# A PEER layer on one core: 64 of 320 tokens leave TensorE's down stage, their rows of v are gathered by GpSimd's indirect DMAs and summed by VectorE

## The reference

```python
q = (xt @ peer_w_q).reshape(PEER_BLOCK, PEER_HEADS, 2, D_KEY_HALF)
v1, i1 = lax.top_k(einsum('thd,nd->thn', q[:, :, 0], keys1), 16)
v2, i2 = lax.top_k(einsum('thd,nd->thn', q[:, :, 1], keys2), 16)
cand_s = v1[..., :, None] + v2[..., None, :]          # 16 x 16 candidates
best_s, pos = lax.top_k(cand_s, 16)                   # 16 experts, 8 heads
gate = jax.nn.softmax(best_s, axis=-1)
act = jax.nn.gelu(einsum('thkd,td->thk', peer_u[idx], xt))
return einsum('thk,thkd->td', gate * act, peer_v[idx])
```

## Time and profile before

| | |
|---|---|
| time before | 1413.51 us, median of 3 runs (1412.66 to 1414.91) |
| the profiled execution | 1415.16 us, its span 1413.4 us |
| busy, TensorE matmul | 1376.3 us, 97% of the span, 11325 instructions |
| busy, VectorE | 991.8 us, 70% |
| busy, ScalarE | 684.1 us, 48% |
| busy, GpSimd | 506.5 us, 36% |
| DMA | 168.69 MB, mean 119 GB/s |
| granted TensorE clock, mean | 0.997 |

### The profile page before, as it was taken

How to read it: one execution, slowest core, us unless ns; L and a number is a source line. 1 busy time by engine, 2 the same in 40 slices (tenths; PEclk the granted TensorE clock), 3 DMA queues, 4 the chain that set the end, 5 groups by cost and what they waited for, 6 DMA issues and landing times.

```text
span 1413.4 us, 34628 instructions
## 1 busy us (share of the span) xinstructions
PE 1376.3 (97%) x11325; PEld 1313.6 (93%) x11325; DVE 991.8 (70%) x2303; ACT 684.1 (48%) x1454; POOL 506.5 (36%) x672
## 2 busy tenths in 40 slices
PE   8999999989999999999999999999999999999996
PEld 6977787788999999999999999999999999999995
DVE  5348777767699995888888888856555555555556
ACT  4665544324445666444444444444444444444444
POOL 5000022302649998766666666652000000000000
PEclk9999999999999999999999999999999999999998
DMA  4343110013414545544444444445555555554553
GB/s 139 120 141 93 50 57 3 3 39 135 135 62 141 141 140 142 134 120 119 119 119 121 122 120 119 119 135 150 149 150 149 150 148 149 148 148 148 148 149 96
DMA packets 85288, 168.69 MB, mean 119 GB/s; under 512 B 9914, under 2 KB 11466, under 8 KB 85034
## 3 DMA queue, kind: packets, MB, share of 16 engines
q1 hardware_dynamic: 85226, 167.84, 40.8%
HBM read 164.80 MB, written 2.97 MB: 119 GB/s over the span
## 4 chain that ended last, share of the span: by engine, by line
PE 84%; POOL 5%; DVE 4%; issue 4%; ACT 2%; DMA 1%; SPq 0%; POOLq 0%; DVEq 0%; ACTq 0%
PE PS L1055 23%; PE PS L1057 22%; PE PS L1056 22%; POOL hlo L642 5%; PE PS L1488 5%; PE PS L1151 1%; PE PS L1335 1%; PE PS L1337 1%; PE PS L1320 1%; PE PS L1443 1%; PE PS L1050 1%; PE PS L1062 1%; DVE wlo L1570 1%; DVE XF L1570 0%; DVE states L1570 0%
## 5 line engine op out<-in xcount | busy, mean ns | idle before, releaser
L642 POOL TENSOR_TENSOR hlo<-hraw,hhiq 128x256 fp32r<-128x256 f32 x512 | 397.8, 787 | 144.8 <-ACT hhiq L690 142.6
L1055 PE MATMUL PS<-H1h,hhiq 128*128 128x320 f32 x1024 | 343.8, 336 | 3.4 <-POOL hlo L642 3.1
L690 ACT ACTIVATE hhiq<-hraw 128x256 fp32r<-128x256 f32 x508 | 210.9, 417 | 258.1 <-PE PS L1057 230.8
L1057 PE MATMUL PS<-H1h,hlo 128*128 128x320 f32 x1024 | 315.4, 308 | 0.0
L1056 PE MATMUL PS<-H1l,hhiq 128*128 128x320 f32 x1024 | 315.1, 308 | 0.0
L1057 PE MATMUL PS<-Wh,hlo 128*128 128x320 f32 x1016 | 314.0, 309 | 0.0
L1055 PEld LDWEIGHTS PS<-H1h,hhiq 128*128 128x128 f32 x1024 | 193.6, 189 | 9.3 <-POOL hlo L642 6.8
L1056 PEld LDWEIGHTS PS<-H1l,hhiq 128*128 128x128 f32 x1024 | 193.4, 189 | 0.0
L1057 PEld LDWEIGHTS PS<-H1h,hlo 128*128 128x128 f32 x1024 | 192.2, 188 | 0.0
L1057 PEld LDWEIGHTS PS<-Wh,hlo 128*128 128x128 f32 x1016 | 190.7, 188 | 0.0
L2011 DVE TENSOR_SCALAR oh<-iotak,pair 128x128 f32<-128x128 f32 x320 | 128.2, 401 | 48.4 <-PE PS L1488 43.8
(11 more groups left out here) (342 smaller groups left out, 2644.8 us busy)
## 6 DMA issues: line engine op xcount, KB each, us to landing
hraw<-in_uT SPq DMA_DIRECT2D x256, 256.0 KB, 2.6
hraw<-in_vE SPq DMA_DIRECT2D x254, 256.0 KB, 2.6
wraw<-in_wbig SPq DMA_DIRECT2D x50, 512.0 KB, 3.9
xin<-in_xT SPq DMA_DIRECT2D x4, 336.0 KB, 4.2
out_yT<-XF SPq DMA_DIRECT2D x8, 160.0 KB
ckx<-in_ckT SPq DMA_DIRECT2D x2, 512.0 KB, 6.9
vs<-in_cv SPq DMA_DIRECT2D x1, 768.0 KB, 8.2
out_ko<-kx SPq DMA_DIRECT2D x1, 672.0 KB
```

The costliest lines, as they stand in the source:

```text
L642: nc.gpsimd.tensor_tensor(hlo[q // 2 % 4][:, cols_], hraw[q // 2 % 4][:, cols_], hhiq[q % 4][:].bitcast(F32), ALU.subtract).then_inc(s_hlo ...
L690: return nc.scalar.activation(out, in_, f, **kw)
L1055: mm(out, whi_, xhi, start=start, stop=False)
L1057: return mm(out, wlo_, xhi, start=False, stop=stop)
```

## The change

The 64 decoding tokens (TM = 256 is where they begin) leave W, the grid and the down matmuls. The 128 experts that each of them picked are taken one by one instead.

- **Scores and routing**: the third set of 128 tokens held the last 128 before. Now both halves of the partitions hold the same 64 decoding tokens (two 64-partition matmuls for one), and later heads 0 to 3 are taken from the lower half, heads 4 to 7 from the upper. So 64 columns (HD = 64) of indices cover 64 tokens x 128 experts.
- **Up**: TensorE still computes all 320 columns. ScalarE takes the gelu of 256 columns as before, and that of the other 64 into a buffer `gd`, which its own DMA queue writes to a scratch tensor `gsc` in memory (one DMA of 32 KB for each e, issued one e later). There are 64 grid groups, not 80.
- **Down**: the matmuls have 256 columns. GpSimd gathers the activations with 64 indirect DMAs (one number for each of 128 partitions), and rows of v with 128 more (512 numbers for each partition, two for one index column). VectorE multiplies activation and gate, and from e = 48 on adds a row after four of five expert rows: 64 `scalar_tensor_tensor` of 1024 columns into `Ys`.
- **End**: eight float32 matmuls with a matrix `fold` add the two halves of the partitions of `Ys` into columns 256 to 320 of the PSUM banks.

```diff
+            def rows_of(n):
+                for x in range(2):
+                    nc.gpsimd.indirect_dma_start(vr[n % 4][:, 512 * x:512 * x + 512], None, vE.rearrange("a p c -> (a p) c"),
+                                                 bass.IndirectOffsetOnAxis(vix[x][:, n:n + 1], 0)).then_inc(s_vr[n % 4], 16)
+            pool.wait_ge(s_ys, 1)
...
+            for x in range(4):
+                pool.wait_ge(s_row[x], GELUS_OUT)
+            for n in range(HD):
+                nc.gpsimd.indirect_dma_start(acts[:, n:n + 1], None, gsc.rearrange("e i (t o) -> (e i t) o", o=1),
+                                             bass.IndirectOffsetOnAxis(aix[:, n:n + 1], 0)).then_inc(s_vr[0], 16)
+            for n in range(4):
+                rows_of(n)
             pool.wait_ge(s_down, 2)
...
+            for n in range(4, HD):
+                pool.wait_ge(s_ys, n - 1)
+                rows_of(n)
```

```diff
-                up_ = PS[:, slot % 4, 0:TQ]
-                A(W[:, bass.ds(e, 1), :].rearrange("p a t -> p (a t)") if direct else up_, up_, ACT.Gelu).then_inc(s_gelu, 1)
+                up_ = PS[:, slot % 4, 0:TM]
+                A(W[:, bass.ds(e, 1), :].rearrange("p a t -> p (a t)") if direct else up_, up_, ACT.Gelu)
...
+                A(gd[:, slot % 4, :], PS[:, slot % 4, TM:TQ], ACT.Gelu).then_inc(s_gelu, 1)
+                if not isinstance(e, int) or e > 0:
+                    keep_gelu(e - 1, slot - 1)
+            def keep_gelu(e, slot):
+                act.wait_ge(s_gelu, e + 1)
+                nc.scalar.dma_start(gsc[bass.ds(e, 1)].rearrange("a p t -> (a p) t"), gd[:, slot % 4, :]).then_inc(s_row[slot % 4], 16)
```

```diff
+                            for c in CHUNKS:
+                                ins = mm(out[c, :], QT[:, 2 * h + x, TM:TQ], kst[:, x, :], start=True, stop=True)
...
-                        ins = three(PS[:, 4 * b + kk, 0:TQ], hhv[2 * s + b][:, P * kk:P * kk + P], lo_[:, P * kk:P * kk + P],
+                        ins = three(PS[:, 4 * b + kk, 0:TM], hhv[2 * s + b][:, P * kk:P * kk + P], lo_[:, P * kk:P * kk + P],
                                     Wh[s][:], Wl[s][:], start, stop)
                         if stop:
-                            ins.then_inc(s_fin, 1)
+                            j = 4 * b + kk
+                            mm(PS[:, j, TM:TQ], Ys[:, P * j:P * j + P], fold[:], start=True, stop=True).then_inc(s_fin, 1)
...
+            pe.wait_ge(s_rconst, 2)
+            pe.wait_ge(s_ys, HD + 2)
```

```diff
+            v.memset(Ys[:], 0.0).then_inc(s_ys, 1)
+            with dve.Fori(1, VFROM // 2) as k:
                 for e in range(2):
                     down(k * 2 + e, e)
+            dve.wait_ge(s_vr[0], ACTS_IN[0] + 32)
+            own(tt(coef[:], acts[:], gat[:], ALU.mult))
+            with dve.Fori(1, (NI - VFROM) // VPER + 1) as k:
+                y = 0
+                for x in range(VPER):
+                    down(k * VPER + (VFROM - VPER + x), x % 2)
+                    if x % 5 < 4:
+                        dve.wait_ge(s_vr[y % 4], k * 64 + (ACTS_IN[y % 4] + 32 * (y // 4) - 32))
+                        dve.wait_ge(s_ys, k * 8 + (y - 6))
+                        v.scalar_tensor_tensor(Ys[:], vr[y % 4][:], coef[:, bass.ds(k * 8 + (y - 8), 1)], Ys[:], ALU.mult,
+                                               ALU.add).then_inc(s_ys, 1)
+                        y += 1
```

More of the change, by code:

```diff
@@ L57 @@
 RIT = 4
-NGR = TQ // 4
+TM = TQ - DEC
+NGR = TM // 4
+VFROM, VPER = 48, 10
 GATED, PAIRED, GRID0 = 9, 10, 11
@@ L250, in build @@
         cand = ranked.put("cand", [P, 3, 16, 16])
+        few = Region(BASE + NK * TM * 4, BASE + 134464)
+        rank = few.put("rank", [P, HD])
+        aix = few.put("aix", [P, HD], U32)
+        vix = [few.put(f"vix{i}", [P, HD], U32) for i in range(2)]
+        gat = few.put("gat", [P, HD])
+        acts = few.put("acts", [P, HD])
+        coef = few.put("coef", [P, HD])
+        fold = few.put("fold", [P, HD])
+        mid = Region(BASE + 134464, BASE + 154944)
+        gd = mid.put("gd", [P, 4, DEC])
+        Ys = mid.put("Ys", [P, D])
+        vr = [mid.put(f"vr{i}", [P, D]) for i in range(3)]
+        vr.append(at("vr3", [P, D], BASE + 154944))
+        gsc = nc.dram_tensor("gsc", (NI, P, DEC), F32, kind="Internal").ap()
         routing = Region(hole_at, TAIL)
@@ L423, in build @@
         s_vhi, s_vlo, s_wh, s_wl, s_down = (sem(x) for x in ("s_vhi", "s_vlo", "s_wh", "s_wl", "s_down"))
+        s_row = s_x
+        X_DONE, GELUS_OUT = 16, 16 + 16 * NI // 4
+        s_vr, ACTS_IN = [sem(f"s_vr{i}") for i in range(4)], (16 * HD, 0, 0, 0)
+        s_ys = sem("s_ys")
         s_sum, s_yf = sem("s_sum"), sem("s_yf")
@@ L664, in _ @@
                     lo(k * (4 * RIT) + q, q)
+            def rows_of(n):
[3 more added lines that the diff above has]
+            pool.wait_ge(s_ys, 1)
+            own(nc.gpsimd.memset(fold[:], 0.0))
+            for c in (0, HD):
+                select(fold[:], [[-1, HD]], ALU.not_equal, -c, 1, 1.0)
+            nc.gpsimd.sem_inc(s_rconst, 1)
+            for x in range(4):
[5 more added lines that the diff above has]
+                rows_of(n)
             pool.wait_ge(s_down, 2)
@@ L975, in _ @@
             up_rest(0)
-            with act.Fori(1, GATED) as k:
+            up_rest(1, blank=True)
+            with act.Fori(2, GATED) as k:
                 up_rest(k, blank=True)
@@ L1439, in scores_of_head @@
                     pe.wait_ge(s_scev, h - 2)
-                for u, t0 in enumerate((0, P, TQ - P)):
+                for u in range(3):
                     for x in range(2):
                         out = flat(PS, 512 * (2 + 2 * (h % 3)) + (2 * u + x) * NK, NK)
-                        ins = mm(out, QT[:, 2 * h + x, t0:t0 + P], kst[:, x, :], start=True, stop=True)
+                        if u < 2:
+                            mm(out, QT[:, 2 * h + x, P * u:P * u + P], kst[:, x, :], start=True, stop=True)
+                        else:
+                            for c in CHUNKS:
+                                ins = mm(out[c, :], QT[:, 2 * h + x, TM:TQ], kst[:, x, :], start=True, stop=True)
                 ins.then_inc(s_scp, 1)
@@ L1505, in _ @@
                     pe.wait_ge(s_routed, 2)
-                for tt in range(3):
+                for tt in range(2):
                     ins = nc.tensor.transpose(PS[:, 4 + x, P * tt:P * tt + P],
@@ L1544, in _ @@
                     down(k * 2 + e, e, False, False)
-            for e in range(NI - 2, NI):
-                down(e, e % 2, False, e == NI - 1)
+            down(NI - 2, 0, False, False)
+            pe.wait_ge(s_rconst, 2)
+            pe.wait_ge(s_ys, HD + 2)
+            down(NI - 1, 1, False, True)
             pe.wait_ge(s_onesg, 2)
@@ L1993, in _, with ranks @@
             v.tensor_copy(gsum[:], b3[:, :, 0]).then_inc(s_routed, 1)
+            sides = [(c, slice(4 * i, 4 * i + 4)) for i, c in enumerate(CHUNKS)]
+            def ranks(by):
+                for c, hs in sides:
+                    ins = v.scalar_tensor_tensor(rank[c, :], sel[c, 5, hs, :].rearrange("p h k -> p (h k)"), by,
+                                                 sel[c, 2, hs, :].rearrange("p h k -> p (h k)"), ALU.mult, ALU.add)
+                own(ins)
+            ranks(float(NK))
+            own(v.tensor_scalar(rank[:], rank[:], float(DEC), tok[:, 0:1], ALU.mult, ALU.add))
+            own(v.tensor_copy(aix[:], rank[:]))
+            ranks(2.0 * NK)
+            own(v.tensor_copy(vix[0][:], rank[:]))
+            own(v.tensor_scalar(rank[:], rank[:], float(NK), None, ALU.add))
+            v.tensor_copy(vix[1][:], rank[:]).then_inc(s_ys, 1)
             dve.wait_ge(s_routed, 1)
@@ L2028, in gelu_row @@
                 w = W[:, bass.ds(r + E0, 1), :].rearrange("p a t -> p (a t)")
[L2029 removed]
+                tt(w, PS[:, slot % 4, 0:TM], w, ALU.mult).then_inc(s_gm, 1)
             def step_of(i, slot):
```

27 lines of the change are left out of this document (18 added, 9 removed).

## The result

The changed kernel takes 1408.57 us (median of 12 runs, 1404.84 to 1411.49), the kernel before 1414.86 beside it on the same chips (12 runs): a ratio of 0.9956, with a 95% interval of 0.9948 to 0.9963. The forecast was 1360 in a range of 1336 to 1408. So the kernel is faster, by 6 us where 54 were forecast. The profiled execution took 1408.23 us with a span of 1406.3.

What follows compares the result with a forecast made beforehand. TensorE was taken as the bound, then the refill of v's tiles in the down stage; -28.3 - 16.0 - 13.8 + 1 + 1.7 - 0.3 + 1.7 = -54.0 from 1415.16 gave 1361.2, said as 1360 after the median's offset, range 1336 to 1408.

Steps and rivals of the forecast that it cites:

- rows of 2.88: Down stage: bound by a tile's refill, an expert row takes (4.34 + 1.42)/2 = 2.88 us, against 3.52 before.
- The cost of a narrower matmul: Down matmuls on TensorE: 256 columns take 0.1185 us instead of 0.1467, worth 87 us if nothing else bound.
- It is not free to take it: Down stage, v's tiles: the cover falls from 5.28 to 4.26 us against a refill of 4.34, so the refill binds.
- Down, rows 48 to 127: Rows with sums and gathers: landing 3.3 us, round (2.84 + C + 2.15)/3 with refill C 5.04; mean 3.32 us, -16.0 us.
- Rival 2: Down stage: loads always queue behind a gather, landing 3.9 us, 3.54 us a row, total 1377; 17 in 100.
- The DMA engines have room: Down rows with gathers: 284 GB/s are needed, and 402 were moved where the queues were full.
- The gathers on GpSimd: Down stage: 192 gathers at 1.4 us each, hidden ahead of row 48 and among the sums.
- rival 4: GpSimd becomes the bound ahead of row 48, then at every sum; 1445 us at 2.45 a gather; 15 in 100.
- `ones2`, `H1s` needed only at the end: GpSimd's queue behind the gathers, down stage: these are needed only at the end; no cost was given.
- Rival 3: Down stage: gathers' instructions slow VectorE, +0.4 us on two thirds of its operations, total 1395; 10 in 100.
- There is no clock to win: TensorE in the down stage: the granted clock is already 1.00, the 2.4 GHz level.
- Up and the small ones: Up stage: fewer grid groups -13.8 us, ScalarE +1; elsewhere scores +1.7, transposes -0.3, final fold +1.7.

Runs made afterwards that it cites:

- own_lo_static: own_lo without the 128 gathers of rows of v, the sums reading buffers of zeros: 1322.07 us, ratio 0.9347 to the kernel before.
- narrow_only: Changed kernel without any gather or the sums on VectorE, 256-column down matmuls kept: 1339.38 us, ratio 0.9468 to the kernel before.
- static_rows: Changed kernel without the 128 gathers of v's rows; full-length sums read zeros, activations' gathers kept: 1363.12 us, ratio 0.9632 to the kernel before.
- own_lo: Changed kernel with low parts of v's tiles in four own buffers, so SyncE refills after the subtraction: 1347.15 us, ratio 0.953 to the kernel before.
- plain_rows: Changed kernel with the 128 row gathers replaced by as many plain DMAs of the same size from GpSimd's queue: 1398.75 us, ratio 0.9892.
- own_lo_early: own_lo with H1s additions placed as in h1s_late and sums from row 32 on, two rows in three: 1347.76 us, ratio 0.9529 to the kernel before.
- h1s_late: Changed kernel with the eight H1s additions one by one behind row gathers 4 to 11, without their s_down wait: 1405.71 us, ratio 0.994.

## Why the prediction was wrong

The down stage was to give 42.6 us and took 3.2 more, a miss of 45.8. The experiments split the whole miss of 49 us along the prediction's own terms. By its rows of 2.88 alone the kernel would take 1413.5 - 128 x 0.64 - 9.7 = 1322; the sums add 80 x (3.06 - 2.88) = 14, the activations' gathers 48 x 0.05 = 2, the gathers of v's rows 80 x (3.32 - 3.06) = 21:

| term | predicted | measured | off by |
|---|---|---|---|
| narrow matmuls alone | to 1322 | 1339.4 | +17 |
| sums, gathers of activations, stall at `H1s` | +17 | +23.7 | +7 |
| traffic of the gathers of v's rows | +21 | +45.5 | +25 |

- *The cost of a narrower matmul* was right: 0.119 us, within a half (0.1165 in own_lo_static).
- *"It is not free to take it"* was right in kind: with three halves of 256 columns as cover the refill binds. It was mis-sized, in half by something that no row of a gapless stage could show: a matmul after a wait holds the engine 0.1 us longer. The other half is open. 2.88 us a row measured 3.00, and 3.03 in the first rows, where 2.93 was taken: +14 us over 128 rows. The 0.05 for the activations' gathers was not needed, as narrow_only's first rows take as long without them.
- *Down, rows 48 to 127: the step that failed.* The landing of a tile beside the gathers was the term that was mis-sized. It was taken at 3.3 us as "a gather moves in some half of the time"; it is 3.8 in the median, up to 5.1. The prediction's own formula gives 3.50 us a row with 3.8, 0.18 more than its 3.32. What the formula lacks even without row gathers, the restart among it, adds some 0.1, as static_rows shows (3.18 for 3.06). The measured 3.71 leaves 0.11; the spread of the landing may be its cause, which no run shows. (3.71 - 3.32) x 78 = 30 us. Rival 2 (1377) had the right mechanism, and its landing of 3.9 was nearly the measured one; it was given 17 in 100, and its 3.54 us a row was too low for the same reasons. The round itself is shown by own_lo: with TensorE's use of the tile out of it, a longer landing cost less. By the Trainium skill ("DMA: Bandwidth & Descriptors", section "Issuing engines are not separate DMA queues") the transfers of all queues interleave on the same DMA engines: plain_rows, at 3.4 instead of 2.6, agrees.
- *"The DMA engines have room"* was the tempting error. 250 GB/s at a share of 0.8 is under the 402 GB/s of the earlier trace rows, so there was room for the bytes, and own_lo moved 307. With this mixture the room ends sooner, at 307/0.91 = 337 GB/s by an estimate from own_lo's window. And room in the mean says nothing of how long one tile takes behind others; here the time of one tile was the bound.
- *The gathers on GpSimd*: 1.3 to 1.4 us from one to the next, where 1.4 was taken; hidden ahead of row 48 and among the sums. Right; rival 4's price is out, and own_lo_early shows how near its place was.
- *What was said of GpSimd's queue was incomplete*: "`ones2`, `H1s` needed only at the end" asked who waits for them, not what they do when they come late. Rival 3 had the contention, but put it on the gathers, whose instructions left VectorE's at 0.69; it came from the displaced `H1s`, once, for 6.75 us. TensorE begins row 48 at 1090.95, 155.9 us into the stage where 48 x 2.93 = 140.6 was forecast. Of these 15 us the stall is 6.75, the low clock behind it 1.5, the first row gathers 1.7 (landing 5.1), and the rows at 3.03 make 4.8. "There is no clock to win" held, but there was clock to lose, and the prediction has no term for it.
- *Up and the small ones*: 10.3 us given ahead of the down stage, forecast 13.8 - 1 - 1.7 + 0.3 = 11.4 (the fold's 1.7 lies behind it). The groups begin 1.6 us later, as taken for the scores.

## What to carry to other kernels

When an engine is made faster in a loop that refills buffers, write down the round of one buffer, load, copies and use, and what else will move on the DMA engines at that time; the time of one transfer beside others counts there, not the mean rate. Before adding traffic to such a loop, shorten what a buffer is held for: here four more tile buffers and another semaphore for the load turned a gain of 0.4% into one of 4.7%. A stall also costs what the clock falls by behind it. And an instruction that a semaphore used to pace runs as a block once its engine comes to it late.

## What the runs showed of the hardware

- The first matmul of 256 columns after a wait takes 0.22 to 0.23 us to the next instead of 0.119, at a granted clock of 1.00, after pauses of 0.16 and 0.23 us.
- Eight 128x320 additions on GpSimd in a row (0.82 us each here, 1.30 each in the earlier trace rows) kept one VectorE subtraction of two SBUF inputs from ending for over 6 us; placed apart (h1s_late) they did not. Indirect DMAs on GpSimd left such subtractions at 0.69.
- An indirect DMA of 128 rows of 2 KB occupies GpSimd for 0.94 to 1.87 us, a plain one of the same size for 0.54. The indirect ones landed after 3.9/4.8/6.2 us (min/median/max), the plain ones after 4.0 in the median.
- Plain loads of 256 KB beside these gathers started ScalarE's copy 3.80 us after their issue in the mean, beside half as many 3.22, alone 2.69, at DMA shares of 0.80, 0.70 and 0.57.
- TensorE stood for 9.4 us up to 1035.83 in own_lo_early, and its granted clock was 0.56 from 1030 to 1040 and 0.93 in the next 10 us, against 1.00, the 2.4 GHz level, before and behind. In the changed kernel it stood for 6.75 us up to 1047.65, and its clock was 0.50, the 1.2 GHz level, from 1045 to 1050: matmuls of 256 columns stood 0.213 us apart until 1051.02, and 0.119 after that.
